# A gated-linear-attention layer in fp32: k of every head turned through DRAM and by 32 by 32 blocks, in place of TensorE

## The reference, cut to what matters

```python
lc = jnp.cumsum(chunks(log_a, GLA_DK), axis=2); lend = lc[:, :, -1:]
q_fwd, k_fwd = q * jnp.exp(lc), k * jnp.exp(-lc)
q_bwd, k_bwd = q * jnp.exp(-lc), k * jnp.exp(lc)
scores = jnp.where(past_mask, einsum(q_fwd, k_fwd), einsum(q_bwd, k_bwd))
o = jnp.einsum('bchls,bcshv->bclhv', scores, v)
d_state = jnp.einsum('bcshd,bcshv->bchdv', k * jnp.exp(lend - lc), v)   # sums over the tokens s of a chunk
# a scan over the chunks: s = g_chunk * s + d_state
o = o + jnp.einsum('bclhd,bchdv->bclhv', q_fwd, s_prev)
```

## Time and profile before

| | |
|---|---|
| median of 3 runs | 2171.36 us (2170.52 to 2171.55) |
| profiled execution | 2170.81 us, of which the span is 2169.1 us |
| PE matmul busy | 2139.3 us, 99% of the span, 9858 instructions |
| POOL busy | 1628.3 us, 75% |
| DVE busy | 1405.3 us, 65% |
| ACT busy | 821.5 us, 38% |
| granted PE clock | 0.997 of full speed |
| DMA | 413.14 MB, 190 GB/s over the span |
| ACT's DMA queue (q10) | 34960 packets, 42.54 MB, 5.8% of 16 engines |

### The profile page before, as it was taken

One profiled execution on the slowest core, in us unless ns is written; L12 is line 12 of the kernel. 1 busy time (PEld: TensorE's weight loads), 2 busy tenths in 40 slices (PEclk: granted clock), 3 DMA queues, 4 the chain that ended last, 5 costly groups with the idle time before them and its releaser, 6 DMA issues.

```text
span 2169.1 us, 27736 instructions
## 1 busy us (share of the span) xinstructions
PE 2139.3 (99%) x9858; PEld 1772.6 (82%) x9858; DVE 1405.3 (65%) x1808; ACT 821.5 (38%) x1453; POOL 1628.3 (75%) x1294
## 2 busy tenths in 40 slices
PE   8999999999999999999999999999999999999997
PEld 6888888888888888788888888788888888888886
DVE  6455545654565454388887856657666667978796
ACT  4233434343344332344444433444444422142223
POOL 7646675667566756798898878988888887777784
PEclk9999999999999999999999999999999999999999
DMA  5332365346533666655455468434434587758782
GB/s 179 107 88 79 125 205 157 115 126 200 159 117 119 216 187 210 249 180 197 177 189 180 170 218 342 173 136 148 173 126 175 213 322 300 276 227 353 276 315 115
DMA packets 246665, 413.14 MB, mean 190 GB/s; under 512 B 34208, under 2 KB 177568, under 8 KB 237568
## 3 DMA queue, kind: packets, MB, share of 16 engines
q1 hardware_dynamic: 211568, 368.83, 48.5%
q10 hardware_dynamic: 34960, 42.54, 5.8%
HBM read 278.14 MB, written 133.17 MB: 190 GB/s over the span
## 4 chain that ended last, share of the span: by engine, by line
PE 64%; DVE 2%; DMA 1%; POOL 1%; SPq 1%; ACT 1%; issue 1%; ACTq 0%; DVEq 0%; POOLq 0%
PE ps L1064 12%; PE ps L1065 12%; PE ps L1069 12%; PE ps L1138 6%; PE ps L1139 6%; PE ps L1143 6%; PE ps L797 1%; PE ps L798 1%; PE ps L801 1%; PE ps L771 1%; DMA hop<-stage 1%; PE ps L773 1%; PE ps L772 1%; PE ps L784 1%; PE ps L783 1%; PE ps L787 1%
## 5 line engine op out<-in xcount | busy, mean ns | idle before, releaser
L703 POOL TENSOR_TENSOR w_op<-w_raw,w_op 128x512 fp32r<-128x512 f32 x330 | 480.5, 1468 | 105.7 <-ACT w_op L1160 102.9
L1064 PE MATMUL ps<-x_op,w_op 128*128 128x512 f32 x1232 | 480.5, 390 | 2.9 <-DVE u L1881 2.5
L1065 PE MATMUL ps<-x_op,w_op 128*128 128x512 f32 x1232 | 480.1, 390 | 0.0
L691 POOL TENSOR_SCALAR ring_hi<-raw 128x512 fp32r<-128x512 f32 x256 | 175.8, 687 | 278.1 <-issue 141.1
L694 POOL TENSOR_TENSOR ring_lo<-raw,ring_hi 128x512 fp32r<-128x512 f32 x256 | 352.1, 1376 | 21.3
L1160 ACT ACTIVATE w_op<-w_raw 128x512 fp32r<-128x512 f32 x330 | 202.8, 627 | 375.9 <-POOL w_raw L721 154.3
L1069 PE MATMUL ps<-x_op,w_op 128*128 128x512 f32 x1232 | 329.9, 390 | 0.0
L1064 PEld LDWEIGHTS ps<-x_op,w_op 128*128 128x128 f32 x1232 | 231.5, 188 | 52.3 <-issue 4.3
L1069 PEld LDWEIGHTS ps<-x_op,w_op 128*128 128x128 f32 x1232 | 231.7, 188 | 48.3 <-POOL w_op L703 0.2
L1065 PEld LDWEIGHTS ps<-x_op,w_op 128*128 128x128 f32 x1232 | 231.5, 188 | 47.9
L1138 PE MATMUL ps<-w_op,hid 128*128 128x512 f32 x616 | 240.7, 391 | 1.5 <-issue 0.7
(11 more groups left out here) (221 smaller groups left out, 4075.2 us busy)
## 6 DMA issues: line engine op xcount, KB each, us to landing
hop<-stage SPq DMA_DIRECT2D x154, 512.0 KB, 2.9
hid<-hop SPq DMA_DIRECT2D x70, 1024.0 KB, 9.3
raw<-in_gla_w_in SPq DMA_DIRECT2D x192, 256.0 KB, 3.3
w_raw<-in_ffn_w_gu SPq DMA_DIRECT2D x176, 256.0 KB, 4.0
w_raw<-in_ffn_w_down SPq DMA_DIRECT2D x88, 256.0 KB, 4.5
xop<-x_stage ACTq DMA_DIRECT2D x42, 512.0 KB, 4.2
x_op<-xop SPq DMA_DIRECT2D x36, 512.0 KB, 8.9
raw<-in_gla_w_out SPq DMA_DIRECT2D x64, 256.0 KB, 3.2
```

The costliest lines, as they stand in the source:

```text
L691: pool.tensor_scalar(ring_hi[:, u, :], raw[:, p, u % 2, :], 1.0, 0.0, ALU.mult, ALU.add).then_inc(unit_hi, 1)
L703: pool.tensor_tensor(shaped(q, tile[:, 1, :]), source(q, i), shaped(q, tile[:, 0, :]).bitcast(F32), ALU.subtract).then_inc(op_ready[i], 1)
L1064: pe.matmul(out, w_hi, x_op[i][:, m, 0, :], start=m == 0 and i < 3, stop=False, skip_group_check=i > 2)
L1065: pe.matmul(out, w_hi, x_op[i][:, m, 1, :], start=False, stop=False, skip_group_check=i > 2)
```

## The change

PE's four transposes per head go. ACT stores kf to DRAM in four DMAs, one for each 32 channels, each with 512 runs of 32 numbers (128 bytes), so that 32 by 32 blocks have changed places; when the four have landed it loads the whole back (256 KB, rows of 2 KB) into `k_back`, DVE turns the blocks inside (`kt`), ACT makes `k_hi`, DVE `k_lo`. `k_back` lies where k_hi lies and `kt` where k_lo lies, so the load waits for the last `d_state` product of the head before. PE no longer waits for `k_lo` before the q columns. In the fourth head DVE scales the next block's first tile under the output and not before v. One semaphore serves both DMAs of og.

```diff
+        k_back, kt = (sb(n, k_at + 4 * T * m, [P, T]) for m, n in enumerate(("k_back", "kt")))
+        k_kept = nc.dram_tensor("k_kept", [P, T], F32)
@@ sync: store_og, load_og
-                sp.wait_ge(og_stored, 16 * (2 * b + hd + 1))
+                sp.wait_ge(og_moved, 16 * (5 * (2 * b + hd) + 1))
@@ tensor: make_scores, and the loop over the heads
                 pe.wait_ge(k_scaled, 2 * (n + 1))
-                for t in range(NT):
-                    tok = slice(t * P, (t + 1) * P)
-                    ins = pe.transpose(ps[:, 0, tok], kf[:, tok], ident[:, :])
-                ins.then_inc(kt_done, 1)
...
-                    pe.wait_ge(k_tok_done, n + 1)
                     column_units(i + 3, 0, ps[:, 0, :])
@@ scalar: head
-                act.wait_ge(kt_done, n + 1)
-                split_hi(k_hi[:, :], ps[:, 0, :]).then_inc(k_hi_done, 1)
+                act.wait_ge(k_scaled, 2 * n + 1)
+                for j in range(4):
+                    act.dma_start(k_kept[:, :].rearrange("(i s) (t j r) -> j s t i r", i=4, t=4, j=4)[j],
+                                  kf[32 * j:32 * j + 32, :].rearrange("s (t i r) -> s t i r", t=4, i=4))\
+                        .then_inc(k_moved, 16)
...                  (the copies of the past scores)
+                act.wait_ge(k_moved, 16 * (5 * n + 4))
+                if n > 0:
+                    act.wait_ge(ds_done, NT * n)
+                act.dma_start(k_back[:, :], k_kept[:, :]).then_inc(k_moved, 16)
                 act.wait_ge(scores_ready, 2 * (n + 1))
                 split_hi(scores_hi[:, :, :], scores[:, :, :]).then_inc(scores_hi_done, 1)
                 under_vr()
+                if hd < H - 1 or b == NB - 1:
+                    turned_k_hi(n)
+            def turned_k_hi(n):
+                act.wait_ge(k_turned, n + 1)
+                split_hi(k_hi[:, :], kt[:, :]).then_inc(k_hi_done, 1)
             def square_next(b):
...
+                    if t == 2:
+                        turned_k_hi(b * H + H - 1)
                     square(SQUARES[b, "ahead"], t, xs[:, t, :], NT)
@@ vector: head (k_lo was made first of all before)
                 split_lo(scores_lo[:, :, :], scores[:, :, :], scores_hi[:, :, :]).then_inc(scores_split, 1)
-                under_vr()
+                if hd < H - 1:
+                    under_vr()
+                dve.wait_ge(k_moved, 16 * 5 * (n + 1))
+                dve.transpose(kt[:, :], k_back[:, :]).then_inc(k_turned, 1)
+                dve.wait_ge(k_hi_done, n + 1)
+                split_lo(k_lo[:, :], kt[:, :], k_hi[:, :]).then_inc(k_tok_done, 1)
+                if hd == H - 1:
+                    under_vr()
@@ vector: side work of the fourth head
                 def next_under_vr():
                     norm_next(b)
-                    scale_next(b, 0)
                 def next_under_o():
+                    scale_next(b, 0)
                     scale_next(b, 1)
                     scale_next(b, 2)
```

More of the change, by code:

```diff
@@ L104, in gla_layer @@
         qf, qb, kf, kb = (qk_scaled[:, n, :] for n in range(4))
+        k_at = MIX + 4 * (2 * KD * T + H * T + 4 * T + 2 * T)
+        k_back, kt = (sb(n, k_at + 4 * T * m, [P, T]) for m, n in enumerate(("k_back", "kt")))
         softlog = qk_scaled
@@ L197, in gla_layer @@
             sem(n) for n in ("k_scaled", "vr_done", "v_hi_done", "v_done", "r_silu", "r_done"))
-        kt_done, k_hi_done, k_tok_done, past_done, future_done, past_copied, scores_ready, scores_hi_done, scores_split \
-            = (sem(n) for n in ("kt_done", "k_hi_done", "k_tok_done", "past_done", "future_done", "past_copied",
+        k_turned, k_hi_done, k_tok_done, past_done, future_done, past_copied, scores_ready, scores_hi_done, scores_split \
+            = (sem(n) for n in ("k_turned", "k_hi_done", "k_tok_done", "past_done", "future_done", "past_copied",
                                 "scores_ready", "scores_hi_done", "scores_split"))
@@ L203, in gla_layer @@
                              "oT_lo_done"))
-        og_stored, og_loaded, oT_blocks = sem("og_stored"), sem("og_loaded"), sem("oT_blocks")
+        og_moved, oT_blocks = sem("og_moved"), sem("oT_blocks")
+        k_moved = sem("k_moved")
         wo_done, wo_added = sem("wo_done"), sem("wo_added")
@@ L513, in store_og @@
                 sp.wait_ge(og_done, NT * (b * H + hd + 1))
-                sp.dma_start(og_kept[:, :].rearrange("(t p) c -> p t c", p=P), og[:, :, :]).then_inc(og_stored, 16)
+                sp.dma_start(og_kept[:, :].rearrange("(t p) c -> p t c", p=P), og[:, :, :]).then_inc(og_moved, 16)
             def load_og(b, hd):
-                sp.wait_ge(og_stored, 16 * (2 * b + hd + 1))
+                sp.wait_ge(og_moved, 16 * (5 * (2 * b + hd) + 1))
                 by_32 = og_kept[:, :].rearrange("(m s) (i c) -> i s m c", s=32, i=4)
                 for i in range(4):
-                    sp.dma_start(og_by_32[32 * i:32 * i + 32, :, :], by_32[i]).then_inc(og_loaded, 16)
+                    sp.dma_start(og_by_32[32 * i:32 * i + 32, :, :], by_32[i]).then_inc(og_moved, 16)
             for b in range(NB):
@@ L1777, in head @@
                 i = b * ROUNDS + 3 * hd
-                dve.wait_ge(k_hi_done, n + 1)
-                dve.nop(nofuse=True)
-                split_lo(k_lo[:, :], ps[:, 0, :], k_hi[:, :]).then_inc(k_tok_done, 1)
                 dve.wait_ge(future_done, n + 1)
@@ L1827, in turn_o_blocks @@
             def turn_o_blocks(b, hd):
-                dve.wait_ge(og_loaded, 16 * 4 * (2 * b + hd + 1))
+                dve.wait_ge(og_moved, 16 * 5 * (2 * b + hd + 1))
                 for j in range(2):
@@ L1940, in next_under_vr, with next_under_o @@
                     norm_next(b)
+                def next_under_o():
                     scale_next(b, 0)
-                def next_under_o():
                     scale_next(b, 1)
```

## The result

The changed kernel takes 2196.76 us (median, 2191.0 to 2200.16), the kernel before beside it 2170.94 us (2169.03 to 2171.55): ratio 1.0122, interval 1.0108 to 1.0136, so 25.8 us slower. The forecast was 2177.6 (6.8 us slower) and the range ended at 2192. The direction was right, the size was not. The profiled execution took 2200.16 us, the longest of the four; its span is 2198.4 us, and the table of before has 2169.1.

The account below looks back on a forecast made before the run. It took PE's own instruction stream (busy 2139 of 2169 us) as the bound. Removed 7.0 - 1.3 for `xf` - 4.5 fourth heads - 8.0 heads 1 and 2 = -6.8 us: 2177.6 us from 2170.8, range 2167 to 2192.

Parts of the forecast that it names:

- the table: Four of heads 1 and 2 in blocks 1 to 3: PE kept waiting at `use_scores`, 8.0 us in all with delay.
- the other two: Remaining two of heads 1 and 2 in blocks 1 to 3: over a microsecond to spare, nothing charged.
- What is removed: PE's four transposes, 0.44 us a head, 7.0 us in all; 1.3 lost to waits for `xf`, at most 5.7 gained.
- The store's load on the DMA engines: k's 2048 short runs per head take 3.2 us of the 16 DMA engines, between 1.6 and 6.4.
- ACT idle before `scores_hi`: Sign of the forecast: ACT stands idle ahead of `scores_hi`, where its wait for the four stores was placed; no size given.
- landing in 4 to 5 us: Sign of the forecast: the stores of k land in 4 to 5 us; over 7 would mean Rival 3.
- Rival 3: Stores of k: a short write pays twice, landing 3.2 us later in 8 to 9 heads; 34 us slower, 2205; chance 0.10.
- Block 0 and the moved scaling: Block 0's heads 0 to 2 cost nothing and gain 0.44 us each; the moved scaling is hidden by 0.4 us.
- The fourth heads: Fourth heads of blocks 0 to 2, no q columns as cover: 0.75, 1.9 and 1.9 us lost, together 4.5.
- x_stage will be later, I take 1.0 us of delay: Heads 1 and 2 of blocks 1 to 3: `x_stage` stores behind the load back, 1.0 us later (ends -0.4 and 3).
- the first sign: PE at least 7 us less busy and its idle time up by 10 or more, in waits of `use_scores`.
- wrong in another place: If PE waits for a weight unit because DMA contention starves POOL's ring; nothing was charged for it.

Follow-up runs that it names:

- e4: Kernel before, with only the next block's first scaling moved from before v to under the output: 2168.05 us, ratio 0.9995.
- e5: Kernel before, PE still turning k, with the four short-run stores of kf added, waited for only before Silu, nothing loaded back: 2172.69 us, ratio 1.0012.
- e2: Changed kernel, but k stored in rows of 2 KB instead of 128-byte runs, leaving out the exchange of blocks: 2178.15 us, ratio 1.0039.
- e1: Changed kernel, but the load back reads unwritten weights, so ACT waits for the stores only ahead of Silu; k is wrong: 2175.24 us, ratio 1.0026.
- e3: Changed kernel, with 91 unread products filling PE's waits at `use_scores` in the eight heads that wait: 2194.31 us, ratio 1.0103.
- e11: As e10, but with all 16 heads turning k through DRAM, block 3's heads 0 to 2 included: 2193.76 us, ratio 1.0113.
- e10: Changed kernel, but SP's queue issues the load back (fourth heads: ACT, behind the first square); PE turns k in block 3's heads 0 to 2: 2184.22 us.
- e6: Changed kernel, with turn, `k_hi` and `k_lo` ahead of the last `x_stage` piece in heads 0 to 2 of blocks 1 to 3; wait kept: 2197.52 us.
- e7: As e6, with wait and load back behind `scores_hi` and the first `x_stage` piece (fourth heads: behind the first square): 2180.33 us, ratio 1.0043.
- e8: As e7, with k stored in rows of 2 KB, leaving out the exchange of blocks: 2176.83 us, ratio 1.0026.
- e9: Changed kernel with the DRAM route only in block 0's first three heads and the very last; PE turns k in the other twelve: 2172.22 us, ratio 1.0008.
- e12: As e10, but POOL issues the load back in place of SP: 2184.96 us, ratio 1.0075.

## Why the prediction was wrong

The heads can be set against its steps one by one: the time from one kf to the next (DVE's L1725, L1706 before), after less before. The forecast's column is what it charged less the 0.44 us gained. Each value is from one execution of each kernel and can be off by some 1.5 us: that is what head 0 of e4 and of e5 shows, where next to nothing was changed.

| heads | forecast, net us each | measured |
|---|---|---|
| 0, 1, 2 | -0.44 | -0.5, -0.5, -0.4 |
| 3, 7, 11 (fourth) | +0.3, +1.5, +1.5 | +0.8, +1.2, +2.7 |
| 4, 8, 12 (first of blocks 1 to 3) | 0 | +0.1, +0.5, +2.6 |
| 5, 10, 13, 14 (the table) | +0.5, +1.0, +2.7, +2.2 | -0.1, +4.3, +3.7, +6.0 |
| 6, 9 ("the other two") | -0.4 | +4.5, +3.4 |
| 15 and what follows | -0.4 | +0.9 |

- *What is removed.* Right: 64 instructions, 0.44 us in each head where nothing else is late, and the wait for `xf` went to 2.3 us as forecast.
- *The store's load on the DMA engines.* Charged with 3.2 us a head, and 1.6 was the lower end: e5 measured 1.6. The two signs "ACT idle before `scores_hi`" and "landing in 4 to 5 us" held (4.0 in the median). Rival 3 is false in its mechanism: 2205 was not far off, but it needed 6.4 us a head and landings of over 7 us, and the runs show 1.6 and at most 6.8. The Trainium skill (DMA: Bandwidth & Descriptors, Specifications) has it that pieces under 512 bytes miss line rate; the direction agrees, as e2's rows of 2 KB issue and land faster (0.44 and 2.9 us against 0.65 and 4.0).
- *Block 0 and the moved scaling.* Right (the first three rows above, and e4).
- *The fourth heads.* Their sum was close, 3.3 net against 4.7, but in part by luck. In block 0 PE starts `use_scores` with next to no wait, and the 0.8 us are lost behind it, in a wait of 1.3 us for the state (183.1) that the forecast did not have. In the other two PE waits 2.37 us for `v_lo`, and in the last the 1.7 us of the clock are in the 2.7.
- *The step that failed: "x_stage will be later, I take 1.0 us of delay", with nothing charged to the other two heads.* In block 2's head 2 the forecast had the last `x_stage` split end at 575.8 without the delay; PE's arrival there shifted by 9.1 us for the earlier losses, so 584.9. It ended at 587.2: 2.3 us of delay, not 1.0. From there to PE's permission (the end of Silu) were 6.75 us and not 6.2. So PE waited 2.92 us, where 1.4 was charged. For the two heads that were charged nothing (6 and 9), these are the last split and PE's start in the kernel before, and then the last splits after (PE's starts after are shown above):

```profile
354.77 1.08 DVE L1606 TENSOR_TENSOR x_stage<-xf,x_stage 128x512 fp32r<-128x512 f32 x1 [1.32 <-ACT x_stage L1160]
...
363.86 0.28 PE L771 MATMUL ps<-v_hi,k_hi 128*128 128x256 f32 x1
...
532.58 0.69 DVE L1606 TENSOR_TENSOR x_stage<-x_sum,x_stage 128x512 fp32r<-128x512 f32 x1 [0.58 <-ACT x_stage L1160]
...
541.96 0.28 PE L771 MATMUL ps<-v_hi,k_hi 128*128 128x256 f32 x1
```
```profile
358.22 1.15 DVE L1625 TENSOR_TENSOR x_stage<-xf,x_stage 128x512 fp32r<-128x512 f32 x1 [0.55 <-ACT x_stage L1163]
...
541.64 1.09 DVE L1625 TENSOR_TENSOR x_stage<-x_sum,x_stage 128x512 fp32r<-128x512 f32 x1
```

With them the forecast's arithmetic can be done for all six heads, as it stands in the prediction. "Late" is its figure without any delay (negative is spare), "delay" the time from kf to the end of the last split, after less before:

| head | late | delay in after | late and delay | PE's wait | delay in e1 |
|---|---|---|---|---|---|
| 5 | -0.1 | -0.1 | -0.2 | 0 | 0.1 |
| 6 | -1.1 | 4.0 | 2.9 | 3.17 | 0.5 |
| 9 | -1.8 | 3.8 | 2.0 | 2.75 | 1.2 |
| 10 | 0.4 | 2.3 | 2.7 | 2.92 | -0.7 |
| 13 | 2.1 | 0.2 | 2.3 | 2.48 | -0.7 |
| 14 | 1.6 | 3.0 | 4.6 | 4.43 | 1.6 |

The fourth column meets the waits to within 0.8 us. So the chain was read rightly, and the term for the delay was mis-sized: 2.2 us in the mean and between -0.1 and 4.0, where 1.0 was taken for four heads and nothing for the two that lost the most by it. With the measured delays the six heads come to 14.5 us and not 8.0. The delay has two parts: `scores_hi` starts 1.6 us later behind kf in the mean (0.1 to 3.3), as the fourth store landed 6.8 to 8.8 us after kf and not 5.6, and from there to the second piece of `x_stage` it is 5.5 us and not 4.5. e1 takes away the first part alone, and the delay falls to 0.3 us in the mean. The first heads of blocks 1 to 3 were not free either: the delay is 3.0, 3.3 and 5.5 us there, and in block 3 it is more than the cover, so PE waits 2.21 us.

- *What was missing altogether: the clock.* No line of the forecast charged anything for TensorE's lower level after a stall. It is 10.2 us of PE's busy time in the profiled execution, and the reason why PE is not 7 us less busy, as the first sign wanted, but 4.3 us more. Within the changed kernel it goes into the time: in head 10 the wait of 2.92 less 0.44 gained leaves 2.5, and the head lost 4.3, 1.8 more; in head 14, 4.43 less 0.44 leaves 4.0, and it lost 6.0. In heads 7 and 12, where no fall follows the wait, the loss is 0.7 less and 0.4 more than the wait leaves. With the 6.5 us of the delays, these 10.2 and the 2.2 of head 12, the forecast's 6.8 becomes, as an estimate, 25.7 of the 29.3 us between the two profiled executions. What would be had back without the clock's fall is less certain: e3 took away 6.8 us of it, and its time is 2.5 us less, with intervals that overlap. The Trainium skill (TensorE: Matmul & The Clock Gate, Why this matters for your kernels) says that idle gaps between bursts of matmuls bring the clock down. This trace agrees in direction for six of eight gaps of 2.2 us and more; four of the six are shorter than the gaps of which the page speaks, and there the measurement decides. The forecast itself had a wait of 3.1 us in block 3 and charged nothing behind it.
- *Block 3.* The forecast saw the full DMA engines there and charged net 4.9 us for two heads; the three heads lost 12.3, of which some 3.4 are the clock's (the falls behind 781.25 and 826.66). e11 against e10 gives 9.5 us for k's traffic and its chain in block 3, and e1 loses 7.8 there even without the wait, partly in the way named as "wrong in another place": PE waits for a weight unit.

What is shown: the wait's place is worth 17.2 us (e6 against e7) to 21.0 (e1); the length of the runs 18.1 in the order of the change, where ACT stands behind them (e2), and 2.0 where it stands behind them later (e8 against e7, with intervals that overlap); block 3 some 8. These overlap and are not to be added. What stays open: how much of the 7 to 9 us left in e7 and e8 is crowding of the DMA engines and how much the longer order of ACT and DVE; and why e9's 1.3 us did not last, for which the waits named there are no more than a candidate. The executions of one kernel also go with their clock: after took 2191.0 us at 0.996 and 2200.16 at 0.992. (1 - clock) times the time is 8.8 us in the one and 17.6 in the other, about the 9.2 us between them; that the clock makes the difference, and not that longer stalls bring more falls, is not shown. Even the faster one is 20 us behind the kernel before. None of the kernels beat the one before.

## What to carry to other kernels

Before putting a wait for a DMA on an engine in order, list everything behind it on that engine, and follow the delay to the end of that list: here 0.44 us a head was taken from TensorE, and some 2.5 us of standing still was put ahead of ACT's whole chain. Heads that seem to have a microsecond or two to spare should be costed with the spread of such a delay and not with one middle value: here it was -0.1 to 4.0 us in six heads of the same make. And when the bound is a TensorE busy for 99% of the time, a stall of some 2 us and more should be charged more than its length, since the clock can fall behind it: by 1.7 us each here.

## What the runs showed of the hardware

- Issuing a store from ACT's queue takes longer with more and shorter runs: 0.65 us in the median for 512 runs of 128 bytes (up to 2.3), 0.44 for 32 rows of 2 KB of the same 64 KB.
- A store of 64 KB in 128-byte runs landed in 4.0 us in the median, in 2-KB rows in 2.9 (e2); the short runs took 1.6 us of 16 engines per 256 KB (e5).
- After six waits of PE of 2.37 to 4.43 us the granted clock was below 1.00 in the next 3 to 6 us (0.67 and 0.76 in the stretches shown), which cost some 1.7 us each; after two others, of 2.21 and 2.37 us, it stayed at 1.00. In e3 it also fell after a wait of 1.84 us, and in e10 two waits of 5.15 and 4.71 us cost 3.4 us each. Products that kept PE busy through the wait kept the clock at 1.00 (e3, seven heads).
- In block 1's second head, the load back was issued 12.7 us after kf from SP's queue (e10) and 13.8 us from POOL's (e12), each behind what stood ahead of it in its order; from ACT's it was 7.0.
